# Output projection of a one-core hybrid decoder layer, changed from four plain column chunks to seven products per half

## What is computed

```python
D_MODEL, SEQ, MIX_WIDTH = 2048, 512, 2048
h = rms_norm(x, g_pre[layer])
proj = jnp.einsum('bsd,de->bse', h, w_in[layer])
...
y = jnp.concatenate([merge_heads(out_a) * jax.nn.silu(ga),
                     merge_heads(out_b) * jax.nn.silu(gb),
                     merge_heads(out_m) * jax.nn.silu(gm)], axis=-1)
o = jnp.einsum('bse,ed->bsd', y, w_out[layer])
x = x + rms_norm(o, g_post[layer])
```

## Time and profile before

| what | value |
|---|---|
| median of 3 runs | 935.07 us (935.0 to 935.89) |
| the profiled execution | 936.1 us |
| its traced span | 934.3 us |
| granted TensorE clock, mean | 0.993 |
| busy: PE, DVE, ACT, POOL | 97%, 70%, 51%, 8% of the span |
| DMA moved | 113.42 MB, mean 121 GB/s |

### The profile page before, as it was taken

The page is one execution under the profiler, slowest core; times in us unless marked ns, Lnnn a source line. Parts: engine busy times, 40 slices in busy tenths (PEclk is TensorE's granted clock), DMA queues, the critical chain, the costliest instruction groups (busy, mean ns, idle before and its releaser), DMA issues.

```text
span 934.3 us, 16316 instructions
## 1 busy us (share of the span) xinstructions
PE 901.8 (97%) x6619; PEld 856.4 (92%) x6619; DVE 649.8 (70%) x940; ACT 474.3 (51%) x862; POOL 79.0 (8%) x71
## 2 busy tenths in 40 slices
PE   8997998999999999999999999999999799999996
PEld 5887998999999999999999999999999788888885
DVE  4889978888777777777777777777777653532324
ACT  5786555555545455555555554546464552541311
POOL 0000508600000000000020201011110000000000
PEclk9999999999999999999999999999999999999999
DMA  9951424343334333343434352525252717632016
GB/s 301 290 137 46 127 78 102 102 115 102 102 102 103 102 102 102 103 105 99 114 91 120 85 136 72 148 66 145 70 136 82 260 65 284 234 91 68 0 47 224
DMA packets 155312, 113.42 MB, mean 121 GB/s; under 512 B 6041, under 2 KB 137145, under 8 KB 154086
## 3 DMA queue, kind: packets, MB, share of 16 engines
q1 hardware_dynamic: 154950, 111.34, 41.9%
q10 hardware_dynamic: 288, 1.05, 0.4%
HBM read 104.22 MB, written 9.73 MB: 122 GB/s over the span
## 4 chain that ended last, share of the span: by engine, by line
PE 81%; DVE 10%; ACT 4%; issue 3%; DVEq 0%; POOL 0%; ACTq 0%; POOLq 0%
PE d_ps L540 12%; PE d_ps L542 12%; PE d_ps L541 12%; PE e_ps L540 6%; PE e_ps L542 6%; PE e_ps L541 6%; PE c_ps L540 3%; PE c_ps L542 3%; PE c_ps L541 3%; PE pt_ps L688 3%; DVE ring L1208 3%; PE score_ps L541 2%; PE score_ps L540 2%; PE score_ps L542 2%; DVE sums L1237 2%
## 5 line engine op out<-in xcount | busy, mean ns | idle before, releaser
L1208 DVE TENSOR_TENSOR ring<-sums,ring 128x1024 fp32r<-128x1024 f32 x112 | 140.4, 1255 | 95.7 <-ACT ring L859 95.0
L540 PE MATMUL d_ps<-tok_hi,ring 128*128 128x256 f32 x672 | 191.2, 285 | 2.9 <-DVE ring L1208 2.9
L542 PE MATMUL d_ps<-tok_lo,ring 128*128 128x256 f32 x672 | 190.1, 283 | 0.0
L541 PE MATMUL d_ps<-tok_hi,ring 128*128 128x256 f32 x672 | 190.1, 283 | 0.0
L1208 DVE TENSOR_TENSOR ring<-raw,ring 128x1024 fp32r<-128x1024 f32 x100 | 124.5, 1249 | 45.2 <-ACT ring L859 45.2
L540 PEld LDWEIGHTS d_ps<-tok_hi,ring 128*128 128x128 f32 x672 | 128.9, 192 | 3.3 <-issue 3.3
L859 ACT ACTIVATE ring<-sums 128x1024 fp32r<-128x1024 f32 x112 | 117.9, 1052 | 22.0 <-DVE sums L1237 20.4
L541 PEld LDWEIGHTS d_ps<-tok_hi,ring 128*128 128x128 f32 x672 | 129.0, 192 | 0.0
L542 PEld LDWEIGHTS d_ps<-tok_lo,ring 128*128 128x128 f32 x672 | 128.9, 192 | 0.0
L859 ACT ACTIVATE ring<-raw 128x1024 fp32r<-128x1024 f32 x100 | 105.2, 1058 | 37.5 <-PE d_ps L542 37.5
L1208 DVE TENSOR_TENSOR wout_split<-raw,wout_split 128x1024 fp32r<-128x1024 f32 x32 | 39.1, 1224 | 71.8 <-ACT wout_split L859 71.2
(11 more groups left out here) (279 smaller groups left out, 2281.0 us busy)
## 6 DMA issues: line engine op xcount, KB each, us to landing
raw<-in_w_in_dram SPq DMA_DIRECT2D x112, 512.0 KB, 5.5
raw<-in_w_out_dram SPq DMA_DIRECT2D x32, 512.0 KB, 5.6
raw<-in_w_mem_kv_dram SPq DMA_DIRECT2D x16, 512.0 KB, 8.3
stage<-in_x_dram SPq DMA_DIRECT2D x4, 1024.0 KB, 9.2
xres<-in_x_dram SPq DMA_DIRECT2D x4, 1024.0 KB, 8.3
out_dram<-o_sb SPq DMA_DIRECT2D x16, 256.0 KB, 3.3
y_dram<-ybuf SPq DMA_DIRECT2D x15, 256.0 KB, 2.3
y_f<-y_dram SPq DMA_DIRECT2D x15, 256.0 KB, 5.2
```

The lines of the kernel that those rows point to most:

```text
L540: pe.matmul(dst, lhs[0], rhs[0], start=start, stop=False, skip_group_check=True)
L541: pe.matmul(dst, lhs[1], rhs[0], start=False, stop=False, skip_group_check=True)
L542: return pe.matmul(dst, lhs[0], rhs[1], start=False, stop=stop, skip_group_check=True)
L1208: return dve.tensor_tensor(dst, a_, hi_.bitcast(F32), ALU.subtract)
```

## The change

The output projection, too, is done by one level of Strassen's scheme. The output columns fall into two groups g of 1024, each of two halves of 512; the tokens into two halves of 256, the channels into two halves of 1024. Per group there are seven products i, each in four steps j (two channel tiles each). The 56 entries (g, i, j) of `STEPS` are called step 0 to step 55 here. A step is 2 token blocks x 2 tiles x 3 = 12 passes of 512 columns, so there are 672 passes.

- **y operands.** Seven sums or parts of y, each 128 x 2048 elements per operand, are loaded to, summed in and split in the places of the token operands. Six are loaded (`load_y`), and four sums are made by DVE (`add_y`); each of the seven is split by ACT (`hi_y`) and DVE (`lo_y`). `y_work(n)` puts this work into ACT's and DVE's lists behind the weights of step n+3.
- **Weights.** A step's weights take the ring of three slots of the main part, under the same rule. Products A and the base of B are loaded (`first_w`, `other_w`), D and G are plain pieces in `raw`, C is a sum by DVE (`add_out`), and B, E and F are made by DMAs issued by POOL that add a 512 KB piece of `w_out` to what lies in `other_w` or `first_w` (`add_piece`, `accum_op=ALU.add`): 24 adding DMAs beside 32 plain ones.
- **Results.** ACT seeds two banks with minus product A (`out_taken`), keeps minus B (`out_five`) and A+C (`out_six`), DVE subtracts or adds these (`out_less_six`, `out_last`). `square` reads the bank for the sum of squares, and `gain` multiplies the bank by `g_post` straight into `o_sb`, so the ACT copy to `o_sb` is gone.
- **The end.** The last product (g=1, G) runs its two token blocks one after another. `finish` is called four times on DVE, for token blocks 2, 3, 0, 1, all behind the weights of step 55.
- **Placement.** Many buffers move in SBUF; the wait for `table_stored` moves from the first q strip to the first exponentials.

```diff
+OUT_ORDER = [[TOK_A, TOK_D, TOK_B, TOK_C, TOK_E, TOK_F, TOK_G], [TOK_A, TOK_B, TOK_D, TOK_C, TOK_E, TOK_F, TOK_G]]
+ADDED_BY_DMA = (TOK_B, TOK_E, TOK_F)
...
+            def before_product(g, i):
...
+                if i in (TOK_D, TOK_C):
+                    pe.wait_ge(out_seeded, 2 * (g + 1))
+                if i == TOK_E:
+                    pe.wait_ge(out_six_taken, 2 * (g + 1))
...
+            def hi_out(step):
...
+                elif i in ADDED_BY_DMA:
+                    act.wait_ge((first_added if i == TOK_E else other_added)[j], added_count(g, i))
...
+                if i == TOK_C:
+                    act.wait_ge(used, product_end(g, i))
+                    if g > 0:
+                        act.wait_ge(out_less_six, 2 * g)
+                    for b in range(2):
+                        act.activation(out_six[:, b], out_d[g][b][:], ACTF.Copy).then_inc(out_six_taken, 1)
...
+            for n, (g, i, j) in enumerate(STEPS):
+                if n >= LAST_STEPS:
+                    continue
+                if n % SUBS == 0 and n > 0:
+                    out_taken(*STEPS[n - 1][:2])
+                hi_out(STEPS[n + RING])
+                y_work(n)
+            out_taken(1, TOK_F)
+            hi_out(STEPS[-1])
...
+                if n == 5:
+                    dve.wait_ge(y_landed[TOK_F], 32)
+                    dve.wait_ge(y_raw, NH)
+                    dve.wait_ge(y_sum, 1)
+                    add_y(TOK_C, TOK_B, TOK_F, ALU.add)
+                if n == 6:
+                    dve.wait_ge(y_sum, 2)
+                    lo_y(TOK_B, 5).then_inc(y_ready, 1)
...
+            def finish(m, s, before):
+
+                dve.wait_ge(part_done, len(results) - 2 + max(m - 1, 0))
+                dve.tensor_reduce(sq[:, s:s + 1], part[:, s], AX_X, ALU.add).then_inc(ssq_done, 1)
+                dve.wait_ge(ssq_done, m + 1)
+                rstd(TILES + m, s, before)
...
+            def add_piece(g, i, j):
+
+                tile, added = (first_w, first_added) if i == TOK_E else (other_w, other_added)
+                if i == TOK_B:
+                    pool.wait_ge(other_landed[j], 16 * (g + 1))
+                elif i == TOK_E:
+                    pool.wait_ge(sum_done, out_sum_count((g, TOK_C, j)))
+                else:
+                    pool.wait_ge(lo_done, out_operand((g, TOK_C, j)) + 1)
+                pool.dma_start(as_rows(tile[j]), w_out_piece(g, *OUT_PART[i], j), accum_op=ALU.add).then_inc(added[j], 16)
```

More of the change, by code:

```diff
@@ L523, in _ @@
[L523 to L530, removed]
-                if s + 2 < QB:
-                    sp.dma_start(xres[:, s % 2], x[0, P * (s + 2):P * (s + 3), :]).then_inc(xres_landed[s % 2], 16)
@@ L536, in _ @@
+            for n, s in enumerate((2, 3, 0, 1)):
+                for j in range(OCH):
+                    sp.wait_ge(final_done, OCH * n + j + 1)
+                    sp.dma_start(out[0, P * s:P * (s + 1), S * j:S * (j + 1)], result_tile(s, j)
+                                 ).then_inc(out_stored, 16)
+            sp.wait_ge(out_stored, 16 * OCH * QB)
         @block.tensor
@@ L810, in _, with out_passes @@
-            for c in range(OCH):
-                if c == 0:
+            def out_passes(g, i, j, b, bank):
+                w = out_slot((g, i, j)).rearrange("p h (e n) -> p h e n", e=2)
+                hi, lo = token_operand(i)
+                cols = slice(P * b, P * (b + 1))
+                for e in range(2):
+                    k = 2 * j + e
+                    last = three(bank[b][:], (hi[:, k, cols], lo[:, k, cols]), (w[:, 0, e], w[:, 1, e]),
+                                 i in (TOK_A, TOK_B) and k == 0, k == KH - 1)
+                return last
@@ new lines, in _ @@
+            for n, (g, i, j) in enumerate(STEPS):
+                if n >= LAST_STEPS:
+                    continue
+                if n % SUBS == 0 and n > 0:
[4 more added lines that the diff above has]
+            hi_out(STEPS[-1])
+            for m, s in enumerate((2, 3)):
+                root(m + 1, s, source=ssq_done)
+            for b in range(2):
+                square(1, TOK_G, b)
+                root(3 + b, b, source=ssq_done)
@@ new lines, in add_y, with last_gated @@
+            def add_y(i, one, two, op):
+                dve.tensor_tensor(token_f32(i), token_f32(one), token_f32(two), op).then_inc(y_sum, 1)
+            def last_gated():
+                dve.wait_ge(pv_done, NH)
+                dve.wait_ge(gate_ready, 2 * NH)
+                dve.wait_ge(used, OPERANDS)
+                for i, cols in ((TOK_D, slice(0, T2)), (TOK_G, slice(0, T2)), (TOK_F, slice(T2, S))):
+                    last = dve.scalar_tensor_tensor(out=token_f32(i)[:, LAST_TILE], in0=pt_ps[0][:, cols], scalar=0.5,
+                                                    in1=gate[:, cols], op0=ALU.mult, op1=ALU.mult)
+                last.then_inc(y_raw, 1)
```

625 lines of the change are left out of this document (409 added, 216 removed).

## The result

| what | before | after |
|---|---|---|
| median | 935.48 us (4 runs) | 974.55 us (4 runs, 971.19 to 975.66) |
| the profiled execution | 936.1 us | 973.84 us |
| its span | 934.3 us | 972.1 us |
| granted clock, mean | 0.993 | 0.972 |

The account below looks back on a forecast made before the run. PE was taken as the bound (busy 97% of the span); passes -21.8, start -4.1, losses 8.1, 4.6, 1.0, 0.4 and 5.7 gave -6.1 us, and 928.9 (said 929) as median. Own range 925 to 932.5; for 8 in 10, up to 938.

Parts of the forecast that it names:

- the adding DMAs: Adds for B, E, F: 3 us each (1.5 to 5.6), hidden behind the passes up to 4.3 us each.
- adds too slow: Rival at E and F, both groups: PE waits for hi; 5.6 us per add gives 944.5 us; chance 0.14.
- have more time: Adds for B: start near 750 us, due from 764 to 776, so no cost.
- the rival's own formula: Eight adds for E and F at 5.6 us, less 34 us of cover: 10.8 in group 1; 4.8 in group 0.
- the clock: Rival: one fall costs 1.7 us, within range; falls at steps 8, 14, 16, 44 up to 6.7, about 935; chance 0.08.
- The rest of the walk: Output projection timed forward from its start to the span's end, adds hidden: 928.0 us, median forecast 928.9.
- DVE's list: Steps 5 to 16: DVE late, lo of step 15 out at 796.4; loss 8.1 us, longest wait 3.5 at step 8.
- Start: Start of the projection: PE's first pass at 743.8 us, 744.1 in effect instead of 748.2; gain 4.1 us.
- DVE beside POOL: POOL's issuing slows DVE from 765 to 800 us: taken as nothing; as rival 5 us, 933.9, chance 0.12.
- C to E: Before product E, PE waits for ACT's copies of A + C: 2.3 us per group, loss 4.6.
- The end: After product F of group 1 (901.7 us): 4.9 us, four finishes 18.3, then 3.1; tail loss 5.7 us.
- the sum -21.8 - 4.1 + 8.1 + 4.6 + 1.0 + 0.4 + 5.7: Passes, start, DVE's list, C to E, step 55's lo, markers, tail: -6.1 us, from 934.3 to 928.2.

Follow-up runs that it names:

- the kernel with room 2048: The changed kernel with dynamic_dma_scratch_size (room for descriptors of POOL's DMAs) 2048 instead of 1024, nothing else; 933.6 us, ratio to before 0.9983.
- with the x loads later: The changed kernel with dynamic_dma_scratch_size 2048 and four x loads moved behind product E of group 1; 932.57 us, ratio to before 0.9968.

## Why the prediction was wrong, step by step

**The failed step: the adding DMAs.** The prediction took 3 us for an add "since an add reads and writes its target", with ends of 1.5 and 5.6 us. It counted bytes. What decided is how many fit in POOL's ring at once: one. So the price of an add was its whole way from issue to landing, about 6.1 us alone and up to 11.5 beside other transfers; even the lower of these is above the upper end. The rival "adds too slow" had the place and the sign right (ACT waits for E and F, PE behind it), gave 944.5 and had a chance of 0.14. It was too mild by 30 us. Of these, 4.7 are what the kernel with room 2048 misses the forecast by (933.6 against 928.9). The rest can be read from one list of moments, the kernel after against the one with room 2048:

| moment | room 2048 | after | late by |
|---|---|---|---|
| copies of A + C, group 0 | 800.90 | 811.79 | 10.9 |
| copies of minus B, group 1 | 859.43 | 879.87 | 20.4 |
| copies of A + C, group 1 | 882.04 | 911.80 | 29.8 |
| lo of step 55 | 909.65 | 950.49 | 40.8 |
| end of span | 931.2 | 972.1 | 40.9 |

First, B: its adds "have more time", said the prediction. They are the queue's head, and the first three of group 0, 7.7 to 9.5 us each beside SP's loads, were late too: 10.9 us by the copies of A + C in group 0, before which no hi of E had waited for an add. Second, 6.1 instead of 5.6, and up to 11.5 where SP moves data. By the rival's own formula, 8 x 6.1 - 34 is 14.8 in group 1, and 8.8 in group 0; measured were 20.4 (from 20.4 to 40.8, with the collisions) and 9.5 (from 10.9 to 20.4), 29.9 together where the rival had 15.6. What a late hi ahead of the copies of A + C cost on top, no run shows: PE waits 12.3 us for them in group 1, but the adds went on at their own pace meanwhile, and the last chain of this execution goes from hi of step 46 straight to the adds of F, not through the copies. Of the 40.9 us, 30.2 are idle time of PE (77.5 against 931.2 - 883.9 = 47.3) and 10.7 are slower passes (PE busy for 894.6 instead of 883.9 us with the same 6525 instructions): the clock, which the prediction had as a rival of its own, came on top of the late adds and not in their place.

**The rest of the walk**, read in the kernel with room 2048, came 4.6 us out (933.6 against 929.0). DVE's list and the first finish of that kernel:

```profile
795.55 1.22 DVE L1422 TENSOR_TENSOR ring<-other_w,ring 128x1024 fp32r<-128x1024 f32 x1
...
910.79 0.15 DVE L1892 TENSOR_REDUCE sq<-part 128x1 f32<-128x4 f32 x1
...
915.13 0.15 DVE L1892 TENSOR_REDUCE sq<-part 128x1 f32<-128x4 f32 x1
```

- *Start.* First pass at 743.8 forecast. In the kernel after:

```profile
743.68 0.50 PE L668 MATMUL d_ps<-ring,tok 128*128 128x512 f32 x1 [2.00 <-DVE tok L1781]
```

- *DVE's list.* Lo of step 15 is out at 795.55 + 1.22 = 796.77; forecast 796.4. PE's wait at step 8 was 3.2 us for 3.5 forecast. Right, though two errors cancel in it: the list starts at 764.63 instead of 765.6, and it waits 3.6 us for hi of step 11 instead of 1.8.
- *DVE beside POOL.* Right at nothing. In the kernel after, while POOL issues adds, the lo of the weights takes as long as in the earlier trace rows, and nowhere near the 1892 of the earlier trace rows; groups by form, 740 us to the end:

```profile
L1422 DVE TENSOR_TENSOR ring<-raw,ring 128x1024 fp32r<-128x1024 f32 x27 | 33.0, 1223 | 37.5 <-ACT ring L1013 37.5
```

- *C to E.* 2.3 each forecast, 2.2 and 3.0 measured. But in group 0 of this trace the clock fell behind the wait, which cost 1.1 more (with the x loads later it did not, behind the same wait).
- *The clock.* The prediction left one fall to its range, at 1.7 us. With room 2048 it fell twice, behind the wait at step 8 and behind the one before E:

```profile
768.00:772.00 4.00, 0.79 (x4) 0.36 (x3) 4.00 (x4) 1.98 (x2) 0.00 (x0) 1.00 1.05 318
772.00:776.00 4.00, 4.00 (x11) 3.10 (x11) 2.01 (x2) 2.15 (x5) 1.20 (x1) 0.57 1.06 344
```

11 passes instead of 19 in the second of these windows are 1.8 us; with the 1.1 at 804, 2.9 of the 4.6 us are named, although the first fall lies under DVE's list in part. The rest is the wait at 880 to 884 in group 1, 3.0 us instead of 2.3, and adds that still come late: ACT waits 4.2 us for those into `sums` even here, and the median with the x loads moved is 1.0 lower. How it divides is not settled.
- *The end.* First finish forecast at 901.7 + 4.9 = 906.6, measured 910.79: the delay from before, no new one. The finishes are 4.34 us apart instead of 4.6, and from the first to the span's end it is 20.4 us for 21.4 forecast. Right to 1 us.

So of the sum -21.8 - 4.1 + 8.1 + 4.6 + 1.0 + 0.4 + 5.7 the terms that the trace lets one read held within 1 or 2 us; the falls of the clock came beside them. What failed was put at nothing, since at 3 us each the adds would hide: a queue that can hold one.

## What to carry to other kernels

Where a change moves work to a queue that the trace of before never shows in use, ask first how many requests the queue holds, and price both cases: the rate when several are in flight and the whole latency when one is. A constant that no one had reason to look at (here the same 1024 in both kernels, harmless while POOL issued no DMA) can decide the sign. And look at what stands in an engine's list behind an instruction with a new wait: two copies that PE needs stood behind such a hi. With room 2048, moving them ahead of it took PE's waits there from 2.2 and 3.0 us to 1.2 each.

## What the runs showed of the hardware

- An adding DMA of 512 KB from HBM to SBUF has 272 packets and takes POOL 1.20 us to issue; a plain one has 144 and takes 0.72. At room 1024 one adding DMA is in flight, or three of 144 packets; at 2048 three adding ones, at 2624 four. With room 2048 and few other loads beside them, the last five of eight started 2.8 us apart in the mean.
- With one in flight, an add started 6.0 to 6.3 us after the one before where little else was moved, and up to 11.5 (with the x loads later 12.7) beside SP's loads.
- A wait of 2 to 3 us did not always cost a fall of the clock. Behind the 2.2 us before product E of group 0 the granted clock was 0.68 with room 2048 and 1.00 with the x loads later. With room 2048 PE was busy for 0.97 of 4 us from 880 on, and the clock stayed at full speed (2.4 GHz) in the next window, while it fell behind the wait at 768 with 0.79 busy:

```profile
880.00:884.00 4.00, 0.97 (x5) 0.71 (x5) 1.84 (x4) 2.03 (x3) 1.24 (x2) 1.00 1.16 229
884.00:888.00 4.00, 4.00 (x19) 3.32 (x18) 1.24 (x3) 1.06 (x1) 1.15 (x1) 1.00 1.02 331
```
